# Diagonals of expert coefficients: from ScalarE's scaled copies to one two-factor VectorE instruction each

## What is computed

```python
qh = (ht @ p['pk_w_q']).reshape(t, PK_HEADS, 2, PK_DH)
s = jnp.einsum('thpd,phkd->pthk', qh, p['pk_sub_keys'])
sv, si = lax.top_k(s, PK_TOPK)                    # 16 best of 128, twice
best, pos = lax.top_k(cand, PK_TOPK)              # 16 best of the 256 sums
gate = jax.nn.softmax(best, axis=-1)
...
act = jax.nn.gelu(jnp.einsum('td,thkd->thk', hb, u_tab[eb]))
return jnp.einsum('thk,thkd->td', gb * act, v_tab[eb])
```

## Time and profile before

| | |
|---|---|
| median of 3 runs | 4265.8 us (4264.91 to 4271.66) |
| the profiled execution | 4269.28 us, span 4267.2 us |
| PE matmul | 3688.6 us busy, 86% |
| VectorE (DVE) | 2605.5 us, 61% |
| ScalarE (ACT) | 1080.1 us, 25% |
| GpSimd (POOL) | 1307.4 us, 31% |
| gathers (indirect DMA) | 1152, 1208.03 MB |
| mean granted TensorE clock | 0.971 |

### The profile page before, as it was taken

How to read it: one execution, slowest core, us unless ns; L and a number is a source line. 1 busy time by engine, 2 the same in 40 slices (tenths; PEclk the granted TensorE clock), 3 DMA queues, 4 the chain that set the end, 5 groups by cost and what they waited for, 6 DMA issues and landing times.

```text
span 4267.2 us, 40396 instructions
## 1 busy us (share of the span) xinstructions
PE 3688.6 (86%) x10642; PEld 1802.4 (42%) x10642; DVE 2605.5 (61%) x6424; ACT 1080.1 (25%) x2672; POOL 1307.4 (31%) x1174
## 2 busy tenths in 40 slices
PE   8999999999997888888898888888888888888776
PEld 3766767555443333333333333333333333333222
DVE  4545455333238677667767766766776677677555
ACT  2534534000002223222222222222222222222211
POOL 0000000000003434444444444444444444444432
PEclk9999999999998999999999999999999999999999
DMA  4010000311429999999999999999999999999998
GB/s 175 16 35 20 25 10 32 129 69 69 182 73 361 420 400 407 420 420 401 413 419 400 420 422 399 421 419 393 421 421 389 420 422 400 417 417 420 413 422 356
DMA packets 187700, 1310.84 MB, mean 307 GB/s; under 512 B 24082, under 2 KB 25618, under 8 KB 36274
## 3 DMA queue, kind: packets, MB, share of 16 engines
q0 software_dynamic: 165888, 1208.03, 68.6%
q1 hardware_dynamic: 21684, 101.33, 6.2%
HBM read 1299.28 MB, written 10.00 MB: 307 GB/s over the span
## 4 chain that ended last, share of the span: by engine, by line
PE 47%; DMA 32%; DVE 9%; issue 9%; ACT 3%; DVEq 0%; POOL 0%; POOLq 0%; SPq 0%; ACTq 0%
DMA arena<-in_uv,arena 32%; PE ps L541 16%; PE ps L1101 9%; PE ps L449 9%; DVE arena L845 3%; PE ps L490 3%; PE ps L473 3%; PE ps L1145 2%; PE ps L1095 2%; ACT arena L636 1%; PE ps L1162 1%; PE ps L1117 1%; DVE arena L791 1%; PE ps L504 0%; DVE arena L795 0%
## 5 line engine op out<-in xcount | busy, mean ns | idle before, releaser
L541 PE MATMUL ps<-arena 128*128 128x512 f32 x4608 | 2201.6, 619 | 471.0 <-ACT arena L636 469.3
L845 DVE CUSTOM_DVE_ANT_0 arena<-arena 128x1024 f32<-128x1024 f32 x1152 | 1409.5, 1226 | 892.5 <-DMA arena<-in_uv,arena 831.4
L415 POOL DMA_INDIRECT arena<-in_uv,arena x1152 | 1301.2, 1130 | 1688.5 <-PE ps L541 1536.2
L541 PEld LDWEIGHTS ps<-arena 128*128 128x128 f32 x4608 | 864.1, 196 | 1723.1 <-issue 885.0
L636 ACT ACTIVATE arena<-ident,arena 128x128 f32<-128x128 f32 x1152 | 398.6, 393 | 1063.1 <-DVE arena L835 1063.1
L1101 PE MATMUL ps<-arena 128*128 128x384 f32 x1152 | 387.8, 493 | 15.9 <-issue 14.0
L406 POOL IOTA arena<- 128x16 f32 x1 | 0.1, 147 | 1244.6 <-DMA x_scratch<-arena 1244.6
L449 PE MATMUL ps<-arena 128*128 128x384 f32 x1152 | 373.9, 487 | 2.2 <-DMA arena<-in_w_mg 2.0
L630 ACT ACTIVATE arena<-arena 128x2 f32<-128x2 f32 x576 | 117.1, 203 | 1001.5 <-DVE arena L845 1001.4
L1101 PEld LDWEIGHTS ps<-arena 128*128 128x128 f32 x1152 | 217.8, 193 | 160.6 <-issue 22.8
L449 PEld LDWEIGHTS ps<-arena 128*128 128x128 f32 x1152 | 218.1, 190 | 159.7 <-issue 6.0
(11 more groups left out here) (200 smaller groups left out, 2438.8 us busy)
## 6 DMA issues: line engine op xcount, KB each, us to landing
arena<-in_w_mod SPq DMA_DIRECT2D x12, 2048.0 KB, 23.3
arena<-in_uv,arena POOLq DMA_INDIRECT x1152, 10.3
arena<-in_w_in SPq DMA_DIRECT2D x28, 512.0 KB, 3.4
arena<-in_w_mg SPq DMA_DIRECT2D x8, 1536.0 KB, 6.2
arena<-x_scratch SPq DMA_DIRECT2D x18, 512.0 KB, 11.7
arena<-in_w_q SPq DMA_DIRECT2D x4, 2048.0 KB, 20.2
arena<-in_xT SPq DMA_DIRECT2D x4, 1152.0 KB, 13.4
arena<-in_x_tok SPq DMA_DIRECT2D x9, 512.0 KB, 4.7
```

The source lines that it names most:

```text
L415: nc.gpsimd.indirect_dma_start(out=RG[:, s, :], out_offset=None, in_=uv, in_offset=bass.IndirectOffsetOnAxis(ap=IDXS[:, par_, s:s + 1], ax ...
L541: mm = nc.tensor.matmul(PS[:, n, :], DG[:, s, :], RG[:, s, D + n * 512:D + (n + 1) * 512], start=False, stop=False, skip_group_check=True)
L845: ins = v.tensor_tensor_reduce(RG[:, s, 0:D], RG[:, s, 0:D], H2C, 1.0, 0.0, ALU.mult, ALU.add, PRE[:, s:s + 1])
```

## The change

VectorE writes each diagonal itself, in one instruction: identity times the GELU column times the gate column. `coef` becomes `diagonals`; ScalarE's diagonals, the columns `COEF` and the semaphore `coef_r` go. The place in VectorE's order is the old one of `coef`, and `next_tile` waits for the diagonals in place of the coefficients.

```diff
-    PRE, GEL, COEF = sm(RING), sm(RING), sm(RING)
+    PRE, GEL = sm(RING), sm(RING)
...
 (ScalarE, rounds)
                     if at in between:
                         between[at]()
-                    act.wait_ge(coef_r, n + 1)
-                    for s in range(g * GRP, (g + 1) * GRP):
-                        A(DG[:, s, :], ident[:], ACT.Copy, scale=COEF[:, s:s + 1]).then_inc(diag_r, 1)
...
 (VectorE)
-        def coef(t, i, q, g):
+        def diagonals(t, i, q, g):
             n = (t * ROUNDS + i * RPP + q) * (RING // GRP) + g
             dve.wait_ge(gel_r, n + 1)
-            sl = slice(g * GRP, (g + 1) * GRP)
-            v.tensor_tensor(COEF[:, sl], GEL[:, sl],
-                            GATE[:, bass.ds(i * RPP * RING + q * RING + g * GRP, GRP)],
-                            ALU.mult).then_inc(coef_r, 1)
+            for s in range(g * GRP, (g + 1) * GRP):
+                v.tensor_scalar(DG[:, s, :], ident[:], GEL[:, s:s + 1],
+                                GATE[:, bass.ds(i * RPP * RING + q * RING + s, 1)], ALU.mult, ALU.mult)\
+                    .then_inc(diag_r, 1)
...
 (VectorE, next_tile)
-            dve.wait_ge(coef_r, (t + 1) * ROUNDS * (RING // GRP))
+            dve.wait_ge(diag_r, (t + 1) * ROUNDS * RING)
```

More of the change, by code:

```diff
@@ L311, in build @@
     gathered = [sem(f"gathered{n}") for n in range(RING)]
-    dots, gel_r, coef_r, diag_r, v_used = (sem(x) for x in ("dots", "gelu_ready", "coef_ready", "diag_ready",
+    dots, gel_r, diag_r, v_used = (sem(x) for x in ("dots", "gelu_ready", "diag_ready",
                                                             "v_used"))
@@ L847, in rounds @@
                     if todo:
-                        coef(t, i, *todo)
+                        diagonals(t, i, *todo)
                         todo = None
```

## The result

The changed kernel took 4290.08 us (median of 5 runs, 4289.37 to 4291.9), the one before 4265.8 (5 runs, 4264.91 to 4271.66): ratio 1.0053, 95% interval 1.0038 to 1.0067. It is slower, by 24 us where 14.5 were forecast, and 3 us above the forecast's own range. The profiled execution took 4289.67 us, span 4287.9, which is 20.7 us more span than before.

What follows compares the result with a forecast made beforehand. The expert part was taken as bound by the DMA gather of 1152 slots, so only lateness where DMA runs short counts: 8.0 + 3.7 + 3.3 - 0.5 = 14.5 us, giving 4280 us; own range 4271 to 4287, 8-in-10 range 4266 to 4306.

Steps and rivals of the forecast that it cites:

- The price per pair: On VectorE, each pair of slots costs 0.445 us more, bounds 0.21 to 0.60; its first diagonal reaches PE about 0.27 us sooner.
- The ordinary tiles: In a half with a pair planned, 3.6 us of added work is covered by 4.9 us of gather waits: no cost.
- Rival 2: VectorE and GpSimd block each other in full, 0.95 us per pair: +35 us, 4301 us; chance 0.13.
- rival 3: Inner loop's body no longer stays loaded, its jump back costs 5.8 us, 15 times: +39 us, 4319 us; chance 0.08.
- Rival 4: Faster: slots set the pace where DMA is short, about 12 ring turns end sooner: -8.4 us, 4257 us; chance 0.05.
- rival 1: Nothing to measure: PE and DMA hide tile 0's lateness, diagonals cost near the lower bound: +3 us, 4269 us; chance 0.12.
- term (b): Tile 0, two stretches where VectorE hardly waits: 3.7 us (1325 to 1390) and 3.3 us (1575 to 1645) uncovered.
- term (a): Six tile boundaries, three pairs each between the last gather wait and the old sum's reading: 6 x 1.33 = 8.0 us.
- the time at which it starts again is set by the first free slot, so all of it shows: At the six boundaries, DMA's restart follows the first free slot, so each 1.3 us of lateness counts in full.
- DMA runs dry no later than before: At the boundaries, DMA's dry spell begins no later, since the tile's last slots are PE's own row of matmuls.
- the signs: What would show the forecast, among it GpSimd's idle time at the six boundaries growing by 1.3 us, from about 11 to 12.3.
- term (c): Time given back by sooner diagonals: 0.27 us at the first of all and 0.27 us at the last ones, -0.5 us.

Runs made afterwards that it cites:

- run 4: Changed kernel, with diagonals written twice from tile 1 on in the two rounds of each call without planning: 4297.13 us, ratio 1.0064 to the kernel before.
- run 1: Changed kernel, with tile 0 the old way (ScalarE's diagonals, VectorE's coefficient step): 4278.65 us, ratio 1.003 to the kernel before.
- run 2: Changed kernel, with the last of each call's four rounds the old way (ScalarE's diagonals): 4283.22 us, ratio 1.0035 to the kernel before.
- run 12: Changed kernel, with only the first calls of tiles 1 to 8 the old way: 4287.86 us, ratio 1.0043 to the kernel before.
- Run 6: Changed kernel, with the old tile's sum read before the new tile's first two dots: 4289.28 us, ratio 1.0048 to the kernel before.
- run 9: Changed kernel, with VectorE's tile loop turned to begin with calls 1 to 3 and end with the next tile's call 0: 4267.24 us, ratio 0.9994 to before.
- run 10: Kernel before, with VectorE's tile loop turned and ScalarE making both coefficients and diagonals: 4246.1 us, ratio 0.9947 to the kernel before.
- run 7: Changed kernel, with the old sum read before the first two dots and no clearing by matmuls of zeros: 4294.27 us, ratio 1.0061 to the kernel before.

## Why the prediction was right and where it was off

**Right: what bounds the kernel, and so the sign.** The price per pair was measured as forecast: 346 ns, 0.26 us from start to start, 0.40 us to PE. The ordinary tiles absorb it; run 4 shows that nearly in full for the light halves, and in calls 1 to 3 of tiles 1 to 7 only 2.4 us more are lost, about the scatter. Rival 2, the mutual block of VectorE and GpSimd, falls with POOL's 1.12 us and the 346 ns; rival 3, a standing still at the inner loop's start, with the waits: 38.4 us in 21 waits for "issue", the six long ones of 5.9 us and no others of that size. Rival 4 falls by the result, and rival 1 by it too: the interval lies above 1.002.

**Off: term (b), tile 0.** It was sized 3.7 + 3.3 = 7.0 us and measured 4.9 in tile 0 and 4.4 in the call behind it, 9.3 together; run 1 gives back 9.8. By stretches, the first call lost 2.0 us more where 3.7 were forecast, and the last call with the one behind it 3.2 + 4.4 = 7.6 where 3.3 were. The first is a misreading: between 1325 and 1390 us the wait for the scores was not the only one worth the name, and the same view of VectorE's waits begins with

```profile
DVE arena L845 <- DMA arena<-in_uv,arena: 1.5, 2, 1.1
```

These waits are gone in the changed kernel, and 3.7 less 1.5 is 2.2. For the second, the step that failed is the end of the stretch at 1645 us: I had ended the account where the planning of the last two pairs ends, and credited a wait of 2.0 us. VectorE's lateness was carried over into tile 1's first call, where `front` and `End` leave it no room, and DMA ran short there, a call that lost only 1.9 us before.

**Right in its sum, partly wrong in its mechanism: term (a), the boundaries.** 8.0 us forecast, 7.4 lost more; by the tiles' lengths it is 9.5. The lateness is there as worked out: PE's clearing starts 1.2 us later after the last wait, and so, on the mean of six, does GpSimd's first issue. Runs 2 and 12 point at the same pairs: tiles 2 to 7 get 3.2 us back when the pairs of each call's last round cost less, in spite of the longer pause, and 0.9 when only those behind the boundary do. Both are differences of single traces. The step that failed is "the time at which it starts again is set by the first free slot, so all of it shows". Run 6 brought the first issue 2.0 us forward for nothing, because the fifth did not move. Nor is the fifth issue the measure: it comes 1.5 us later in the changed kernel than before, and 1.5 later still in run 4, where the first calls lost no more. "DMA runs dry no later than before" failed as well. The last issue ahead of the hole comes 0.8 us later, since PE's last matmuls do, so GpSimd's idle time grew on the mean from 11.4 to 11.8 us, by 0.4 and not by the 1.3 that the signs named. How the 1.2 us turn into lost DMA time is thus open, and the closeness of 8.0 and 7.4 is partly luck.

**The rest of the miss.** 14.5 us forecast; the span grew by 20.7. Of the 6.2 between them, 9.3 - 7.0 = 2.3 are tile 0's, -0.6 the boundaries', 2.4 the ordinary calls', -0.1 tile 8's, 1.8 lie ahead of the expert part, and the 0.4 left are about the term (c), which is too small for any trace here to show. The medians lie further apart, 24.3 us, since the profiled execution before was 3.5 us above its median and the one after was not.

**Open.** The one of the six boundaries that I had read in detail lost no more after the change; the growth is in those into tiles 2 to 4 (1.5, 3.5 and 2.4 us). In the kernel before these had the earlier first issues (26.9 to 27.9 us after the last wait), and those into tiles 5 and 6 the latest (28.6 and 28.5, after a longer pause and at the low clock), so there was less left to add. The one into tile 7 does not fit, with 27.2 us before and only 0.2 us more lost. Why TensorE's clock rose earlier at some of them no run shows. Nor is it settled how much of the 24 us lies at the boundaries: the sum of lost DMA time gives 7.4 us, the tiles' lengths 9.5.

## What to carry to other kernels

With one engine's work hidden behind a stream that another resource sets, ask where the stream runs short and count the added work there, up to the point at which the engine is level again, not up to the first thing that it releases. Work below the cover of a stretch is nearly free, and work beyond it begins to be paid: 1152 extra instructions cost 24 us, the next 1152 another 71. A loop's start that costs a pause can be put where the engine has slack, and that gave 16.6 us in the kernel before and 25 in the changed one, about as much as the question of who writes the diagonals.

## What was not expected of the hardware

- The pause at the start of VectorE's tile loop moves with the loop's start and differs with the body: 5.8 to 5.9 us in the changed kernel, up to 6.6 in run 2, 5.3 to 5.4 in run 9, 4.6 to 4.9 in run 10. The Trainium skill ("Runtime: NRT & Kernel Launch", Instruction fetch mechanics) states that a taken branch out of the two loaded pages has to wait for a fetch. That the pause moves with the loop's start agrees with this as its cause, and no run here shows the fetch itself.
- Matmuls of zeros that look like waste can cover the time at the low clock: without them (run 7) the first real matmuls ran at a granted clock of 0.50, after 8.27 us of standing still, and the kernel was not faster.
- How long that low clock reached into the first slots differed from boundary to boundary in one trace (0.86 and 0.53 granted in the same stretch of tile 1 to 2 and 5 to 6), and the first issue with it by 1.7 us.
- One-input VectorE instructions are stretched now and then at the end of GpSimd's DMA_INDIRECT, but rarely: 30 of the 1152 diagonals took over 400 ns, and 29 of them had such an end inside them. The 689 others that met one took 342 ns on the mean, as did the 403 that met none. The changed kernel's diagonals, shortest, median and longest in ns:

```profile
L832 DVE TENSOR_SCALAR arena<-ident,arena x1152: 320/342/581, 1299.4 to 4274.7; 128x128 f32<-128x128 f32 x192
```

Their mean of 346 ns is 9 above the 337 of the mixer's, where no gather runs.
